# A 1-core transformer chain in fp32: more products by split operands, adaLN loads and accumulations moved

## The chip, the cores and the metric

The kernel runs on 1 core of one Trainium2 chip. Times are device microseconds of one execution; a result is the median of several.

## The reference, cut to what matters

One sequence of 256 tokens, width 1024, all in fp32. First come two layers conditioned on a vector `c`:

```
c_act = silu(c)
for layer in range(2):
    mod = c_act @ ada_w[layer] + ada_b[layer]          # 6 x 1024: shift, scale, gate for mixer and feed-forward
    h = rmsnorm(x) * (1 + scale_m) + shift_m
    mix = conv + retention(h) if layer == 0 else s5(h) # s5: two-way scan, GELU, then (z @ w_glu_a) * sigmoid(z @ w_glu_b)
    x = x + gate_m * mix
    h = rmsnorm(x) * (1 + scale_f) + shift_f
    x = x + gate_f * (relu(h @ w_fc1[layer]) ** 2 @ w_fc2[layer])
x = rmsnorm(x)
```

Then a block with three branches: `proj = rmsnorm(x) @ w_in` gives queries, keys, values and gates for gated linear attention (`gq, gk, gv, gg, ga1`), forgetting attention (`fq, fk, fv, ff`) and attention into a memory (`mq`), and three 1024-wide sigmoid gates `bg`; the gated branches are summed, go through `w_out`, and a SiLU-gated feed-forward of width 2816 follows.

## The kernel before, in words

Activations lie transposed, 1024 features as 8 tiles of 128 partitions by 256 tokens. Weights stream in panels of 2 MB (512 columns of all 1024 rows, or 512 rows of 1024 columns) through a ring of three slots, loaded by SP in the order of `panels`; a panel's load waits until TensorE has finished the panel three before it. TensorE works off one list of jobs, `job_order` (L62), in that order. Jobs write into six PSUM banks in turn, so a job waits until the job six before it has been read; the `ada` jobs share one further bank.

There are two ways to multiply. `project` (L1678) uses plain fp32 operands. `project_split` (L1716) uses operands cut in two fp32r parts, and `three` (L1710) sums high x high, high x low and low x high. For it a *unit* of a panel (128 x 2048 values, half a panel) is cut: ACT copies it into one of three high buffers (`split_high`, L778), VectorE subtracts and leaves the low part in the ring (`split_low`, L1232). A high buffer is free again when the unit three before it has been multiplied, which `split_high` waits for. Before, layer 0's first product (`f1.0.0` to `f1.0.15`), the first two of eight row blocks of its second (`FC2 = 2`, `rows_open`, L1695) and all projections of the last block are plain; the other row blocks (`rows_split`, L1728), GLU, layer 1's feed-forward, the branch outputs and the last feed-forward are split.

Conditioning: `mod` needs 24 column pieces k of `ada_w`, 2 MB each (k = 0 to 11 for layer 0, k = 12 to 23 for layer 1). `ada_load` (L576) brings piece k into one of two slots, from ACT's queue save the first two, which GpSimd issues. `ada_acc(k)` (L1176) multiplies its eight slabs by `c_act` and sums them on VectorE, eight instructions. TensorE's job `ada(k)` (L1759) sums over partitions, and `ada_mod(k)` (L1192) adds the bias into `mod`. `begin` (L1637) makes `ada(k)` wait until `mod` of k-1 is written. Where pieces fall is set by `ADA_AFTER` (L59): pieces 10 to 21 among the 16 jobs of layer 0's first product, 22 and 23 in its second (`side_work`, L1908).

S5 weights are prepared ahead: for each of eight groups GpSimd computes powers (`powers`, L647; 32 operations, then a store), TensorE's jobs `wt{k}.0`, `kl{k}`, `wt{k}.1` (`s5_weights`, L1860) turn them, ACT stores them (`s5_weights_out`, L855). GpSimd begins group k when `wt{k-1}.1` is done. Groups 1 to 4 stand in the first product, 5 to 7 in the second.

Every engine follows its own fixed order and stops at a wait. The orders that the change touches, on VectorE: start (L1258: `ada_acc` 0 to 3, norm, `ada_acc(4)`, `s5_scalars` at L1148, `gated` L1267, `convolve` L1271, `ada_acc(5)`), the adaLN loop of layer 0 (L1358), the loop over row blocks (L1362), the GLU loop (L1433), and in the last block the chain of decays (L1476 to L1506, ended by the job `kot`), `head_norm` (L1508), `gla_out` (L1538) and the eight attention rounds (L1566: logits, maximum, exp on ACT, normalisation). On ACT: `next_ada` (L891), the loop over row blocks (L898), `head_squares` (L1019), `gate` (L1048). In each round TensorE does `us{u}` (logits), a gate unit `bg{u}`, and the transpose `ut{u-1}`; every second round `uo` (values).

Of the kernel before, what the change touches and what calls it, by code (L numbers as in the profile page):

```python
# [20 lines left out]
P = 128  # L21
# [21 lines left out]
SW_ADA = 2  # L43
# [15 lines left out]
ADA_AFTER = {1: 10, 2: 11, 3: 12, 5: 13, 6: 14, 7: 15, 9: 16, 10: 17, 11: 18, 13: 19, 14: 20, 15: 21}  # L59


def job_order():  # L62

    jobs = ["ada0", "ada1", "ada2", "ms0", "ada3", "av0", "ag0", "av1", "ag1", "ada4", "q0", "q1", "cv0", "ada5", "k0", "k1", "ada6",
# [3 lines left out]
    for j in range(16):  # L68
        jobs.append(f"f1.0.{j}")
        if j in ADA_AFTER:  # L70
            jobs.append(f"ada{ADA_AFTER[j]}")
        if j % 4 == 0:
            k = j // 4 + 1
            jobs += [f"wt{k}.0", f"kl{k}", f"wt{k}.1"]
    for b in range(8):
        if b < 2:
            jobs.append(f"ada{22 + b}")
        if b % 3 == 0:
            k = 5 + b // 3
            jobs += [f"wt{k}.0", f"kl{k}", f"wt{k}.1"]  # L80
# [10 lines left out]
    jobs += ["ga0", "ga1", "gb0", "gb1", "ga2", "ga3", "gb2", "gb3", "ms3", "mk0", "mk1"]  # L91
    jobs += ["f1.1.0", "mkr0", "f1.1.1", "mkr1"] + [f"f1.1.{j}" for j in range(2, 16)]
    jobs += [f"f2.1.{p}" for p in range(4)] + ["ms4", "mv0", "ms5", "mv1"]
    jobs += ["gq0", "gk0", "ga1r", "ff", "gv0", "gv1", "la", "gg0", "gg1", "fq0", "fq1", "kot", "cs0", "cs1",
# [34 lines left out]
def build(nc, a, out):  # L129

    ctx = ExitStack()
    with ctx:
# [5 lines left out]
        def s(name):  # L138
            if name not in sems:
# [8 lines left out]
                   ("memory_kv", 2048), ("tabw", 3072), ("ada_acc", 1024)]  # L148
# [12 lines left out]
        prep = sb("prep", 3200)  # L161
# [115 lines left out]
        gates = big3  # L277
# [6 lines left out]
        wsm = early[:, 0:640].rearrange("p (k c) -> p k c", k=8)  # L284
        wa2 = early[0:16, 640:896]
# [88 lines left out]

        base = 0
        FC2 = 2
# [7 lines left out]
        add_units([f"f2.1.{i}" for i in range(8)], 512, high_bufs)  # L384
        base = BRANCH = len(units)
        high_bufs = [split["ada_slot0"][:, 0:2048], split["ada_slot0"][:, 2048:4096], split["big"][:, 24 * T:32 * T]]
# [9 lines left out]
        def unit_parts(u):  # L396

            name, c0, n, buf = units[u]
# [3 lines left out]
            return panel_view(name)[:, :, c0:c0 + n], low[:, :, c0:c0 + n], buf[:, 0:k * n].rearrange("p (k c) -> p k c", k=k)  # L402
# [11 lines left out]
        h_hi = split["squares"][:, :].rearrange("p (k t) -> p k t", k=KT)  # L414
        h_lo = split["h_in"][:, :].rearrange("p (k t) -> p k t", k=KT)
        big_lo = split["big"][:, :].rearrange("p (k t) -> p k t", k=32)

        def fc2_high(b):

            name, o = (("squares", 0), ("squares", 1024), ("memory_kv", 0))[(b - FC2) % 3]  # L420
            return split[name][:, o:o + 1024].rearrange("p (k t) -> p k t", k=4)
# [45 lines left out]
        freed.update({"gq0": ("gqk", 1), "gk0": ("gqk", 2), "ga1r": ("ga1c", 1), "ff": ("ffx", 1), "la": ("lax", 2),  # L467
# [14 lines left out]
        def unit_wait(eng, u):  # L482
# [8 lines left out]
            elif BRANCH <= u < LAST:  # L491
                job_wait(eng, branch_ends[u - BRANCH])
            else:
                first, before = (0, 0) if u < GLU else (SECOND + 16, 7 - FC2) if u < BRANCH else (DOWN, 14 - FC2)
# [4 lines left out]

        last_jobs = [name for name in JOBS if name[:2] in ("fg", "fu")]  # L500
        NORM_G = (("norm_g", 0), ("norm_g", 8), ("norm_g", 16), ("norm_g", 24), ("norm_f", 0), ("g_mix", 0), ("g_ffn", 0))
        NCONST = 6
        NLATE = 8

# [4 lines left out]
        def _(sp):  # L509
            sp.dma_start(cols[:, :], a["cols"]).then_inc(s("cols_in"), 16)  # L510
            sp.dma_start(x, a["x"].rearrange("(k p) t -> p k t", p=P)).then_inc(s("x_in"), 16)

            def load_win(k):
                if k == 0:
                    sp.wait_ge(s("ada_acc"), 2 * ADA)
# [23 lines left out]
            for i, (name, src, k, n, _) in enumerate(panels):  # L539
# [44 lines left out]

        @block.gpsimd
        def _(pool):
            pool.dma_start(prep[:, 0:192], a["s5_scal"]).then_inc(s("s5_in"), 16)
            ada_load(pool, 0)
            ada_load(pool, 1)
            pool.dma_start(ident[:, :], a["ident"]).then_inc(s("const_in"), 16)  # L590
# [23 lines left out]
            pool.dma_start(early[:, 1536:2176], a["rope"]).then_inc(s("const_in"), 16)  # L614
            pool.dma_start(scanmask[:, :], a["scanmask"]).then_inc(s("const_in"), 16)
            pool.dma_start(dreg[:, :], a["decay"]).then_inc(s("const_in"), 16)
            pool.dma_start(s5c[:, :], a["s5_select"]).then_inc(s("const_in"), 16)
# [114 lines left out]
        def _(act):  # L732
# [28 lines left out]
            def shift(n):  # L761

                act.wait_ge(s("mod"), ADA * (n // 2) + (2 if n % 2 == 0 else 8))
                for k in range(KT):
# [3 lines left out]
                    if n == 3 and k:  # L768
                        input_high(k - 1, s("h"), 24)
                if n == 3:  # L770
                    input_high(KT - 1, s("h"), 24)

            def input_high(k, ready, base):

                act.wait_ge(ready, base + k + 1)
                act.activation(h_hi[:, k, :], h[:, k, :], ACT.Copy).then_inc(s("h_high"), 1)

            def split_high(u):  # L778
# [4 lines left out]
                if u == 0:  # L783
                    job_wait(act, "f1.0.15")
                elif u in (1, 2):
# [7 lines left out]
                elif BRANCH <= u < BRANCH + 3:  # L793
# [82 lines left out]
            ada_load(act, 10)  # L876
            squares(1)
            ada_load(act, 11)
            shift(1)

# [10 lines left out]
            def next_ada(j):  # L891
                if j in ADA_AFTER:
                    ada_load(act, ADA_AFTER[j] + 2)
                if j % 4 == 0:
                    s5_weights_out(j // 4 + 1)

            relus(0, next_ada)
            for b in range(FC2, 8):  # L898
                for u in range(2 * (b - FC2), 2 * (b - FC2) + 2):
                    split_high(u)  # L900
                    if u == 2:
                        s5_weights_out(5)
# [4 lines left out]
                if b == FC2 + 2:  # L907
                    s5_weights_out(6)
            s5_weights_out(7)
# [46 lines left out]

            act.dma_start(wsm[:, :, 0:64], a["w_fox_f"].rearrange("(k p) c -> p k c", p=P)).then_inc(s("late"), 16)
# [4 lines left out]
            for p in range(4):  # L962
# [3 lines left out]
                act.activation(tmp3[:, 2 * p:2 * p + 2, :], ps2(f"gb{p}"), ACT.Sigmoid).then_inc(s("glus"), 1)  # L966
            split_high(SECOND)
# [9 lines left out]
            def after_relu(j):  # L977
                split_high(SECOND + j + 3)
                if j == 1:
                    root("mkr0", 512)  # L980
                    root("mkr1", 512)
                act_high(j, 2 * j, s("fsq"), j + 1)
# [1287 lines left out]
```

## Time and profile before

| what | us |
|---|---|
| median of 3 runs | 1395.38 |
| the runs | 1390.31, 1395.38, 1395.55 |
| the profiled execution | 1394.85 |
| its span | 1393.0 |
| TensorE busy | 1269.5 |
| VectorE busy | 735.4 |
| ACT busy | 452.9 |
| GpSimd busy | 370.1 |

The profile is of one execution. PE is TensorE's matmul side, PEld its weight loads, DVE VectorE, POOL GpSimd, SP the queue that loads panels. L1676 is the one line through which nearly all matmuls go, so stages are told apart by time and by the operands' names. A plain fp32 multiplication leaves two records, a split one three.

### The profile page before, as it was taken

What the parts mean: (1) busy time and instruction counts of PE and PEld (TensorE: products, weight loads), DVE (VectorE), ACT (ScalarE), POOL (GpSimd) and SP (SyncE); (2) the same over time, 40 slices, a digit from 0 to 9 for tenths busy, and PEclk for the clock granted to TensorE, in tenths of its full rate; (3) what the DMA queues carried; (4) which work ended last, traced back from release to release, by engine and by line L of the source; (5) the groups of instructions that cost most, each with busy time, mean ns of one, the idle gap of its engine ahead of it and who ended that gap; (6) DMA issues with size and microseconds to landing.
All of it is one profiled execution on the core that took longest, in us unless ns stands there. A gap on an engine that the chain in (4) does not pass through costs nothing.

```text
span 1393.0 us, 22876 instructions
## 1 busy us (share of the span) xinstructions
PE 1269.5 (91%) x9992; PEld 1135.4 (82%) x9992; DVE 735.4 (53%) x878; ACT 452.9 (33%) x619; POOL 370.1 (27%) x581
## 2 busy tenths in 40 slices
PE   1699998888999967888999999999999998899999
PEld 1587687777889947878999999668678898799998
DVE  4897985434363438955586543304542165555353
ACT  2221123111123343434555332114155343444341
POOL 7999653455534607810000000000000011000000
PEclk9899999999999988999999999999999999999999
DMA  8963675897765283426245555333333344355461
GB/s 324 365 216 140 226 258 203 328 340 289 280 228 210 100 314 107 130 73 235 100 175 183 186 186 183 109 108 126 113 122 121 121 149 154 121 182 182 143 220 61
DMA packets 118787, 258.08 MB, mean 185 GB/s; under 512 B 5056, under 2 KB 18656, under 8 KB 118560
## 3 DMA queue, kind: packets, MB, share of 16 engines
q1 hardware_dynamic: 86160, 185.78, 37.9%
q10 hardware_dynamic: 27584, 51.01, 10.0%
q0 software_dynamic: 4944, 19.83, 3.9%
q8 instruction: 79, 1.29, 0.4%
q14 instruction: 20, 0.16, 0.0%
HBM read 241.93 MB, written 14.68 MB: 184 GB/s over the span
## 4 chain that ended last, share of the span: by engine, by line
PE 71%; DVE 12%; DMA 8%; issue 3%; POOL 3%; ACT 3%; ACTq 0%; DVEq 0%; POOLq 0%
PE bank L1676 71%; DMA ada_slot<-in_ada_w 6%; DVE ada_acc L1189 3%; DVE big L1285 3%; POOL big L722 2%; DVE rstd L1199 1%; DMA memory_kv<-s_tables 1%; POOL big L715 1%; DVE ring_split L1236 1%; DVE h_in L1220 1%; ACT ada_slot_split L802 1%; DMA ring<-in_w_ffn_up 1%; DMA ring<-in_w_ffn_down 1%; DMA ring<-in_w_glu_a 1%; DVE ada_acc L1186 0%
## 5 line engine op out<-in xcount | busy, mean ns | idle before, releaser
L1676 PE MATMUL bank<-h_in,ring 128*128 128x256 f32 x1536 | 351.4, 390 | 7.7 <-ACT h_in L767 7.7
L1676 PEld LDWEIGHTS bank<-h_in,ring 128*128 128x128 f32 x1536 | 297.7, 195 | 53.3 <-issue 10.7
L1676 PE MATMUL bank<-squares_split,ring_split 128*128 128x256 f32 x800 | 226.9, 284 | 0.0
L728 POOL TENSOR_TENSOR y_cat<-y_cat,tmp 128x512 f32<-128x512 f32 x8 | 10.7, 1345 | 552.4 <-DVE tmp L1608 552.4
L1676 PEld LDWEIGHTS bank<-squares_split,ring_split 128*128 128x128 f32 x800 | 154.1, 193 | 0.0
L1189 DVE SCALAR_TENSOR_TENSOR ada_acc<-ada_slot,cact,ada_acc 128x512 f32<-128x512 f32 x168 | 134.0, 797 | 5.9
L1676 PE MATMUL bank<-ada_slot_split,ring_split 128*128 128x256 f32 x432 | 122.2, 283 | 0.0
L1236 DVE TENSOR_TENSOR ring_split<-ring,ada_slot_split 128x2048 fp32r<-128x2048 f32 (+1 forms) x24 | 53.9, 2247 | 62.6 <-ACT ada_slot_split L802 62.6
L1676 PEld LDWEIGHTS bank<-ada_slot_split,ring_split 128*128 128x128 f32 x432 | 82.9, 192 | 0.0
L1676 PE MATMUL bank<-h_in_split,ada_slot_split 128*128 128x256 f32 x256 | 74.9, 293 | 8.3 <-DVE y_cat_split L1612 3.8
L1676 PE MATMUL bank<-one,ada_acc 128*128 128x1 f32 x192 | 29.1, 273 | 56.4 <-DVE mod L1194 35.3
L1199 DVE RECIPROCAL rstd<-bank 128x512 f32<-128x512 f32 (+1 forms) x21 | 56.0, 2669 | 43.8 <-ACT bank L746 43.4
L1676 PEld LDWEIGHTS bank<-one,ada_acc 128*128 128x128 f32 x192 | 29.7, 229 | 59.8 <-DVE mod L1194 37.6
L1236 DVE TENSOR_TENSOR ring_split<-ring,tabw_split 128x2048 fp32r<-128x2048 f32 x22 | 50.4, 2291 | 50.2 <-ACT tabw_split L802 50.2
L885 ACT ACTIVATE big<-bank 128x512 f32<-128x512 f32 x32 | 19.1, 598 | 167.2 <-PE bank L1676 167.2
L802 ACT ACTIVATE ada_slot_split<-ring 128x2048 fp32r<-128x2048 f32 (+1 forms) x24 | 44.9, 1876 | 67.6 <-PE bank L1676 41.5
L1676 PE MATMUL bank<-squares_split,tabw_split 128*128 128x256 f32 x208 | 59.0, 284 | 0.0
L1676 PE MATMUL bank<-h_in_split,tabw_split 128*128 128x256 f32 x208 | 58.9, 283 | 0.0
L1676 PEld LDWEIGHTS bank<-h_in_split,ada_slot_split 128*128 128x128 f32 x256 | 51.1, 199 | 9.4 <-issue 8.2
L1676 PE MATMUL bank<-h_in_split,ring_split 128*128 128x256 f32 x192 | 56.1, 292 | 0.0
L1186 DVE TENSOR_SCALAR ada_acc<-ada_slot,cact 128x512 f32<-128x512 f32 x24 | 12.1, 503 | 82.9 <-DMA ada_slot<-in_ada_w 82.9
L802 ACT ACTIVATE tabw_split<-ring 128x2048 fp32r<-128x2048 f32 x22 | 42.0, 1911 | 41.8 <-PE bank L1676 31.7
(391 smaller groups left out, 3084.7 us busy)
## 6 DMA issues: line engine op xcount, KB each, us to landing
ring<-in_w_fc SPq DMA_DIRECT2D x32, 2048.0 KB, 8.2
ada_slot<-in_ada_w ACTq DMA_DIRECT2D x22, 2048.0 KB, 12.4
ring<-in_w_in SPq DMA_DIRECT2D x19, 2048.0 KB, 8.1
ring<-in_w_ffn_gate SPq DMA_DIRECT2D x5, 2048.0 KB, 7.7
ring<-in_w_ffn_up SPq DMA_DIRECT2D x5, 2048.0 KB, 7.8
ring<-in_w_ffn_down SPq DMA_DIRECT2D x5, 2048.0 KB, 7.9
ring<-in_w_out SPq DMA_DIRECT2D x4, 2048.0 KB, 9.1
ring<-in_w_branch SPq DMA_DIRECT2D x3, 2048.0 KB, 7.9
```

Source lines behind the costliest of these rows:

```text
L715: pool.tensor_tensor(wbuf[n % 2], pb[:, 0], pb[:, 1], ALU.add).then_inc(s("s5w"), 1)
L722: pool.tensor_tensor(rotated(m)[:, 1], gbuf[m % 2][:, :, ::-1, :], tab[:, :, 2:0:-1, :], ALU.mult).then_inc(s("s5r"), 1)
L728: pool.tensor_tensor(merged, merged, tmp3[:, 2 * p:2 * p + 2, :], ALU.add).then_inc(s("mga"), 1)
L802: act.activation(high, whole, ACT.Copy).then_inc(s("w_high"), 1)
L885: act.activation(hh, ps2(f"f1.{l}.{j}"), ACT.Relu).then_inc(s("relu"), 1)
L1186: ts(acc, w[:, 0, :], cact[:, 0:1], None, ALU.mult).then_inc(s("ada_part"), 1)
L1189: stt(acc, w[:, i, :], cact[:, i:i + 1], acc, ALU.mult, ALU.add)\
L1199: return dve.reciprocal(rs[:, 0:width], ps(job)[:, 0:width]).then_inc(s(sem), 1)
L1220: stt(dst[:, k, :], x[:, k, :], gain[:, k:k + 1], rs[:, 0:T], ALU.mult, ALU.mult).then_inc(s("hn"), 1)
L1236: tt(low, whole, high.bitcast(F32), ALU.subtract).then_inc(s("w_low"), 1)
L1285: stt(conv[:, i, :], src, w, conv[:, i, :], ALU.mult, ALU.add).then_inc(s("conv"), 1)
L1676: return pe.matmul(*args, skip_group_check=True, **kw)
```

## The change

1. Layer 0's first product and all projections of the last block become split units, the second product leaves one row block plain (`FC2 = 1`). The norms in front of them (`SPLIT_NORMS`) are cut too. `ga1r` and `ff` become one job of 80 rows.
2. The first four adaLN pieces are loaded by SP ahead of the first panel, into the two slots, a part of `big` and ring slot 2; VectorE accumulates six of their slabs, TensorE two. Small loads (`s5_scal`, constants) move from GpSimd's queue to SP's. `ms0` goes ahead of `ada0`.
3. The other pieces are spread: 10 to 15 in the first product, accumulated in halves, 16 to 20 in the second, 21 in GLU, 22 and 23 in layer 1. S5 groups stand after jobs 0, 5, 10, 15 and row blocks 1, 3, 5.

```diff
-SW_ADA = 2
+EARLY_ADA = 4
+DVE_SLABS = 6
...
-ADA_AFTER = {1: 10, 2: 11, 3: 12, 5: 13, 6: 14, 7: 15, 9: 16, 10: 17, 11: 18, 13: 19, 14: 20, 15: 21}
+ADA_AFTER = {3: 10, 6: 11, 8: 12, 11: 13, 13: 14, 15: 15}
+ADA_LOAD_AFTER = {2: 12, 5: 13, 7: 14, 10: 15, 12: 16, 14: 17}
+ADA_HALVES = {0: (10, 0), 1: (10, 1), 2: (11, 0), 4: (11, 1), 5: (12, 0), 6: (12, 1), 7: (13, 0), 9: (13, 1),
+              10: (14, 0), 11: (14, 1), 12: (15, 0), 13: (15, 1)}
+ADA_MOD_BEFORE = {5: 10, 8: 11, 10: 12, 13: 13, 15: 14}
+S5_AFTER = {0: 1, 5: 2, 10: 3, 15: 4}
+SIDE_ADA = {0: 16, 1: 17, 3: 18, 5: 19, 6: 20}
+SIDE_S5 = {1: 5, 3: 6, 5: 7}
...
-        FC2 = 2
+        FC2 = 1
+        T_, B_, Y_ = buffers_at((("tmp", 0), ("big", 6144), ("y_cat", 0)))
+        for i in range(16):
+            units.append((f"f1.0.{i // 2}", 256 * (i % 2), 256, ((T_, B_, Y_) * 4 + (T_, Y_) * 2)[i]))
...
+            for k in range(EARLY_ADA):
+                sp.dma_start(ada_slot(k), ada_source(k)).then_inc(ada_in(k)[0], 16)
...
+                elif u < FC:
+                    job_wait(act, f"f1.0.{u - 3 if u < 13 else u - 2}")
...
-            squares(0, False)
-            for k in range(2, 6):
-                ada_load(act, k)
-            root("ms0")
+            squares(0)
+            act.wait_ge(s("panel0"), 16)
+            ada_load(act, 4)
             shift(0)
+            ada_load(act, 5)
             ada_load(act, 6)
...
             def next_ada(j):
-                if j in ADA_AFTER:
-                    ada_load(act, ADA_AFTER[j] + 2)
-                if j % 4 == 0:
-                    s5_weights_out(j // 4 + 1)
+                if j + 3 < FC:
+                    split_high(j + 3)
+                if j in ADA_LOAD_AFTER:
+                    ada_load(act, ADA_LOAD_AFTER[j])
+                if j in S5_AFTER:
+                    s5_weights_out(S5_AFTER[j])
...
             for b in range(FC2, 8):
                 for u in range(2 * (b - FC2), 2 * (b - FC2) + 2):
-                    split_high(u)
-                    if u == 2:
-                        s5_weights_out(5)
+                    split_high(FC + u)
+                    if u in (4, 8, 12):
+                        s5_weights_out(4 + u // 4)
...
                 act.activation(fc2_high(b), big3[:, 4 * b:4 * b + 4, :], ACT.Copy).then_inc(s("b_high"), 1)
...
+                if 3 <= b < 6:
+                    ada_load(act, 15 + b)
...
             def head_squares(i, name, dst):
...
+                split_high(PROJ + (9, 10, 11, 12, 15, 16)[i])
...
             def gate(j):
...
+                if GATES + j + 3 < BRANCH:
+                    split_high(GATES + j + 3)
...
+            split_low(0)
             residual(0, "wo0", 16)
...
-            for k in range(10, 23):
-                ada_acc(k)
-                if k > 10:
-                    ada_mod(k - 1)
+            for j in range(16):
+                if j + 3 < FC:
+                    split_low(j + 3)
+                if j in ADA_MOD_BEFORE:
+                    ada_mod(ADA_MOD_BEFORE[j])
+                if j in ADA_HALVES:
+                    k, half = ADA_HALVES[j]
+                    ada_acc(k, 4 * half, 4 * half + 4)
+            ada_acc(16)
+            ada_mod(15)
             for b in range(FC2, 8):
-                split_low(2 * (b - FC2))
-                split_low(2 * (b - FC2) + 1)
+                split_low(FC + 2 * (b - FC2))
+                split_low(FC + 2 * (b - FC2) + 1)
...
+                if b == 1:
+                    ada_acc(17)
+                    ada_mod(16)
+                elif b == 2:
+                    ada_acc(18)
+                    ada_mod(17)
+                elif b == 4:
+                    ada_mod(18)
+                    ada_acc(19)
+                elif b == 5:
+                    ada_acc(20)
+                    ada_mod(19)
...
+                if p == 1:
+                    ada_acc(21)
+                if p == 2:
+                    ada_mod(21)
...
+            for u in range(5, 9):
+                split_low(PROJ + u)
             dve.wait_ge(s("ffe"), 2)
...
+                split_low(GATES + u + 3)
...
             for u, name in enumerate(glu_jobs):
                 project_split(name, GLU + u, z_hi, z_lo, (lambda k: pe.wait_ge(s("z_low"), k + 1)) if u == 0 else no_wait)
+                if name == "ga3":
+                    ada(21)
```

## Rows read from the trace of the kernel before

**Rows 1.** Waits of TensorE: engine, line, releaser: us in total, times, longest.

```profile
PE bank L1676 <- DVE mod L1194: 35.3, 7, 11.7
PE bank L1676 <- DVE ada_acc L1189: 21.1, 2, 18.7
```

**Rows 2.** Chain that ended last: start us, us, what, number of records.

```profile
632.57 23.48 PE bank L1676 x192
...
1090.49 8.64 PE bank L1676 x40
...
1326.08 63.60 PE bank L1676 x528
```

**Rows 3.** Windows of three stages: length, PE, PEld, DVE, ACT, POOL busy (records), clock, DMA, GB/s.

```profile
226.40:385.80 159.40, 144.14 (x993) 125.49 (x994) 74.16 (x115) 27.52 (x51) 77.39 (x136) 0.93 0.82 297
385.80:497.20 111.40, 110.92 (x1010) 105.38 (x1011) 50.26 (x45) 34.54 (x30) 50.27 (x67) 0.97 0.48 175
888.50:1122.00 233.50, 230.22 (x1018) 178.49 (x1018) 74.32 (x104) 83.46 (x134) 0.00 (x0) 0.99 0.34 117
```

**Rows 4.** Timeline of VectorE at the start: start us, us, line, operation.

```profile
59.73 0.52 DVE L1186 TENSOR_SCALAR ada_acc<-ada_slot,cact 128x512 f32<-128x512 f32 x1
60.28 5.59 DVE L1189 SCALAR_TENSOR_TENSOR ada_acc<-ada_slot,cact,ada_acc 128x512 f32<-128x512 f32 x7
...
75.60 0.69 DVE L1269 TENSOR_TENSOR big<-bank,big 128x512 f32<-128x512 f32 x1
```

**Rows 5.** The page: bytes moved by slice, DMA issues with us to landing.

```profile
GB/s 324 365 216 140 226 258 203 328 340 289 280 228 210 100 314 107 130 73 235 100 175 183 186 186 183 109 108 126 113 122 121 121 149 154 121 182 182 143 220 61
...
ring<-in_w_fc SPq DMA_DIRECT2D x32, 2048.0 KB, 8.2
ada_slot<-in_ada_w ACTq DMA_DIRECT2D x22, 2048.0 KB, 12.4
```

**Rows 6.** Groups by form of ACT and VectorE: busy us, mean ns, idle before.

```profile
L802 ACT ACTIVATE y_cat_split<-ring 128x2048 fp32r<-128x2048 f32 x15 | 28.7, 1912 | 27.1 <-PE bank L1676 27.1
...
L885 ACT ACTIVATE big<-bank 128x512 f32<-128x512 f32 x32 | 19.1, 598 | 167.2 <-PE bank L1676 167.2
...
L1236 DVE TENSOR_TENSOR ring_split<-ring,y_cat_split 128x2048 fp32r<-128x2048 f32 x15 | 34.5, 2297 | 24.8 <-ACT y_cat_split L802 24.8
```

**Rows 7.** Timeline of VectorE: norm of layer 1, reciprocal and last low parts.

```profile
667.10 1.76 DVE L1199 RECIPROCAL rstd<-bank 128x256 f32<-128x256 f32 x1 [6.11 <-ACT bank L746]
...
675.84 0.76 DVE L1230 TENSOR_TENSOR h_in_split<-h_in,squares_split 128x256 fp32r<-128x256 f32 x2 [0.55 <-ACT squares_split L776]
```

**Rows 8.** Timeline of TensorE in layer 0's first product, behind an adaLN job.

```profile
264.44 9.31 PE L1676 MATMUL bank<-h_in,ring 128*128 128x256 f32 x32
```

**Rows 9.** Chain that ended last, ahead of the S5 scan.

```profile
499.26 16.59 DMA memory_kv<-s_tables
```

**Rows 10.** Timeline of GpSimd: ends of a step, operations that meet other work.

```profile
160.40 1.12 POOL L655 TENSOR_TENSOR tabw<-tabw,early 128x128 f32<-128x128 f32 x2
...
236.60 0.54 POOL L674 DMA_DIRECT2D memory_kv<-in_s_bc  x1 [19.74 <-PE bank L1676]
...
257.09 0.58 POOL L707 DMA_DIRECT2D s_wout<-prep  x1 [0.30 <-POOL prep L660]
...
450.34 2.81 POOL L655 TENSOR_TENSOR tabw<-tabw,early 128x128 f32<-128x128 f32 x2
```

**Rows 11.** Timeline of VectorE in GLU.

```profile
641.85 2.29 DVE L1236 TENSOR_TENSOR ring_split<-ring,ada_slot_split 128x2048 fp32r<-128x2048 f32 x1 [5.28 <-ACT ada_slot_split L802]
```

**Rows 12.** Timeline of ACT around the chain of decays.

```profile
938.50 0.60 ACT L1004 ACTIVATE big<-bank 128x512 f32<-128x512 f32 x1 [6.31 <-PE bank L1676]
...
953.29 0.60 ACT L1030 ACTIVATE tmp<-bank 128x512 f32<-128x512 f32 x1
```

**Rows 13.** Timelines of VectorE and ACT in one attention round.

```profile
1046.70 0.69 DVE L1574 TENSOR_TENSOR tabw<-bank,early 128x512 f32<-128x512 f32 x1 [4.02 <-PE bank L1676]
...
1049.46 1.28 ACT L1052 ACT_TABLE_LOAD   x1
```

More of the change, by code:

```diff
@@ L90, in job_order @@
     jobs.append("z7")
-    jobs += ["ga0", "ga1", "gb0", "gb1", "ga2", "ga3", "gb2", "gb3", "ms3", "mk0", "mk1"]
-    jobs += ["f1.1.0", "mkr0", "f1.1.1", "mkr1"] + [f"f1.1.{j}" for j in range(2, 16)]
+    jobs += ["ga0", "ga1", "gb0", "gb1", "ga2", "ga3", "ada21", "gb2", "gb3", "ms3", "mk0", "mk1"]
+    jobs += ["f1.1.0", "mkr0", "f1.1.1", "mkr1"]
+    for j in range(2, 16):
+        jobs.append(f"f1.1.{j}")
+        if j in (5, 9):
+            jobs.append(f"ada{22 + j // 9}")
     jobs += [f"f2.1.{p}" for p in range(4)] + ["ms4", "mv0", "ms5", "mv1"]
-    jobs += ["gq0", "gk0", "ga1r", "ff", "gv0", "gv1", "la", "gg0", "gg1", "fq0", "fq1", "kot", "cs0", "cs1",
+    jobs += ["gq0", "gk0", "ff", "gv0", "gv1", "la", "gg0", "gg1", "fq0", "fq1", "kot", "cs0", "cs1",
              "nr0", "nr1", "at0", "at1", "fk0", "fk1", "go0", "gor0", "nr2", "nr3", "go1", "gor1",
@@ L160, in build @@
         early = sb("early", 2176)
-        prep = sb("prep", 3200)
+        prep = plain["prep"]
         s5c = sb("s5_select", 656)
@@ L284, in build @@
         wsm = early[:, 0:640].rearrange("p (k c) -> p k c", k=8)
+        wsm_hi, wsm_lo = (split[name][:, o:o + 640].rearrange("p (k c) -> p k c", k=8) for name, o in (("tabw", 2048), ("prep", 2048)))
         wa2 = early[0:16, 640:896]
@@ L981, in after_relu @@
                     root("mkr1", 512)
+                if j == 4:
+                    act.wait_ge(s("late"), 80)
+                    act.activation(wsm_hi, wsm, ACT.Copy).then_inc(s("wsm_high"), 1)
+                if j == 3:
+                    ada_load(act, 23)
+                if j == 8:
+                    act.wait_ge(s("ada_acc"), 24)
                 act_high(j, 2 * j, s("fsq"), j + 1)
             relus(1, after_relu)
-            for u in range(SECOND + 19, BRANCH):
+            for u in range(SECOND + 19, PROJ):
                 split_high(u)
             squares(4)
+            split_high(PROJ)
             job_wait(act, "mv0")
@@ L1183, in ada_acc @@
                     dve.wait_ge(s("cact"), 1)
-                for i in range(KT):
+                for i in range(first, min(end, n)):
                     if i == 0:
@@ L1552, in _ @@
             gla_out(1)
+            for u in range(13, 16):
+                split_low(PROJ + u)
             def fox_rows(hd):
@@ L1786, in _ @@
             pe.wait_ge(s("pool_const"), 6)
-            ada(0)
-            ada(1)
-            ada(2)
             mean_squares(0)
-            ada(3)
+            for k in range(EARLY_ADA):
+                ada(k)
             w, w_ag = panel("av"), panel_view("ag")
```

320 lines of the change are left out of this document (210 added, 110 removed).

## The prediction

> **What bounds the kernel now.** I first read who TensorE waits for [rows 1]: the adaLN vectors (`DVE mod` and `DVE ada_acc`, 56.4 us together) are its largest waits. Next, its pace between waits, from the chain that ended last [rows 2]: 40 records of plain fp32 take 8.64 us, 0.216 each, and a multiplication leaves two, so a 256-column unit (16 multiplications, 32 records) takes 6.91 us; a split one is 48 records of 63.60 / 528 = 0.1205 us, 5.78 us. A conversion gives back 1.13 us a unit. The windows of the stages [rows 3] show layer 0's first product idle for 15.3 us and at 0.93 of the clock, with DMA at 0.82; the second product and block 2's projections have no idle time to speak of. So TensorE bounds nearly everything, save the start (adaLN, then VectorE's convolution) and the S5 scan.
>
> The sum is against the profiled execution, 1394.85 us (span 1393.0 and 1.85 around it), 0.5 us under the median shown.
>
> **Start.** Four adaLN loads go ahead of the first panel on SP's queue, and TensorE takes two of eight slabs of each. What decides is VectorE: ada4's accumulation (6.1 us), S5 scalars, gated values, 46 convolution steps, ada5, which TensorE waits for. Before, that chain starts at 59.73 and reaches the gated values at 75.60 [rows 4]. Now ada4's load is issued when `av` has landed: 11.9 MB are ahead, 33 us at the 365 GB/s of the second slice; 12.4 us for a load beside others [rows 5] gives 46 and the gated values at about 62: **-13** (-8 if loads behind each other are slower, -16 if they land at once). ACT waits for ada4 inside its queue (load 6) until then, with `ag0`'s sigmoid behind it, which is needed only after it. Constants and S5 scalars move from GpSimd's queue to SP's; they are needed 20 us later.
>
> **Into layer 0's feed-forward.** One `split_low`, 2.3 us [rows 6], stands ahead of the residual that frees the bank of `wo0.3`: +2.3. The normed input is now split: in layer 1 the same code goes from reciprocal to last low part in 667.10 to 676.6 [rows 7], so the first job ends 13.4 us behind `ms1`, not 10.8: +2.6. Together **+4.9**.
>
> **Layer 0's products.** Fifteen further units give 15 x 1.13 = 17.0, the converted block (64 fp32 records to 96 split ones) 2.2, three adaLN jobs of 0.85 that move out 2.5: **-21.7**. The old waits and their slow clock go: 15.3 idle, 0.07 x 159 and 0.03 x 111 for the clock [rows 3], **-30**. The unit behind such a wait took 9.31 us, where 6.91 is the pace: behind an idle TensorE the granted clock is the lower of its two levels, 1.2 of 2.4 GHz, for part of the stretch [rows 3, 8]; I count 2.4 us a wait below.
>
> New waits come from order, not load. TensorE's `ada(k)` needs `mod` of k-1 read. VectorE reads it in step j only behind `split_low(j+3)`, whose high half ACT makes after job j: relu 0.6, a square as long, split 1.9, then low 2.3 and the small read, 5.6 us [rows 6]. `ada12` stands directly behind job 8 and mod 11 is read in step 8: 5.6 us. `ada13` stands behind job 11, mod 12 in step 10 behind unit 13, whose buffer only frees after job 11: 1.9 + 2.3 + 0.2 = 4.4. `ada14` stands behind job 13, mod 13 behind unit 15, free after job 13, and half an accumulation (3.1): 7.5. Sum 17.5, and 3 x 2.4 of clock.
>
> The second product has a larger one. VectorE accumulates ada18 after block 2's parts, but ACT issues its load only at the end of its block 3, whose second unit waits for the first half of TensorE's block 2. From there: 1.9 + 1.1, load 8 to 12 [rows 5], accumulation 6.1 [rows 4], `split_low` 2.3: 20 to 23 us, while TensorE has 5.8 us left. Block 3 waits **14.7**, plus 2.4 clock. ada19 and ada20 have a block more in hand: 1.5. New waits: 17.5 + 7.2 + 14.7 + 2.4 + 1.5 = **+43.3**. The net of this stage is only -8.4.
>
> **S5.** Its weights end one block earlier, so its tables no longer queue behind each other; the table that landed after 16.6 us [rows 9] arrives before ACT needs it: **-4.3** (0 if still queued).
>
> GpSimd makes those weights in 20.5 us a step, 236.60 to 257.09; by the sums above the steps now stand 26 to 43 us apart. Two of its operations that meet a `split_low` take 2.81 us, the same two under back-to-back convolution steps 1.12 [rows 10]: about 2 us for each split. So a step with four to five splits takes about 29: **+3.5** over three places (0 to 10). The Trainium skill (Trainium Architecture — The Big Picture, "What this means for kernel authors") calls the port pair of VectorE and GpSimd an exclusive lock, not a shared bandwidth. By that a step would stretch by all of VectorE's busy time and the sum would be 42 us higher; The 1.12 speaks against so strict a reading, the 2.81 for it with long instructions.
>
> **GLU.** `ada21` stands behind `ga3` on TensorE, and its accumulation behind `split_low` of unit 6, whose panel lands late: that split ends at 644.1 [rows 11], gating 2.0, accumulation 6.2: 652.3, with TensorE ready two units after 632.57 [rows 2], at 644.3. +8.0, the job 0.8, clock 2.2: **+11**. ada22 and ada23 cost 1.6 and about 1 of lag in layer 1: **+2.6**.
>
> **Projections and gates.** 22 units give 24.9; the four token-major jobs have 512 columns, for which the trace has no split row: between 0.216 (one fp32 record of 256) and 0.241 (twice 0.1205), 5.2 to 5.8 a job against 6.91; I take 5.3, the column rate, -6.4; `ga1r` and `ff` merge, 7.2 to 2.9. Together **-36** (bounds -38 and -33). Against it:
> - the split input and first units, 1.7;
> - decay chain: `kot` was ready just in time, 13 us after `gg1`; ACT ran from 938.50 to `kot`'s copy at 953.29 [rows 12]. Now a split precedes the exponentials and two more precede that copy, 5.7, and TensorE has 2.3 us less work to cover it: 8 less the 0.6 there was, about 6 with rounding by the splits that overlap;
> - `mq1`, whose unit frees after `fv0`: 1.4;
> - the eight attention rounds. Logits to the end of exp take 2.8 us (1046.70 to 1049.46), the sigmoid table 1.3 [rows 13], sigmoids 0.8. Now ACT's split 1.9 and VectorE's 2.3 come between the gate and the next logits: 9.1 a round, 9.8 with the forget rows, 14 with the head norms; TensorE needs 7.9 to 9.3. Over the eight some 10.5.
>
> So **+19.6**, net -16.4.
>
> Sum: -13 + 4.9 - 8.4 - 4.3 + 3.5 + 11 + 2.6 - 16.4 = -20.1, so **1374.5 us**.
>
> On the pace: the Trainium skill (TensorE: Matmul & The Clock Gate, "Wait — 56ns, not 53.3ns?") gives back-to-back matmuls N / 2.4 GHz plus 2.5 ns, 109 ns at 256 columns. By it the sum would be about 22 us lower; 528 matmuls at 120.5 ns [rows 2] decide.
>
> **Rivals.**
> - *No new waits.* ACT and VectorE stay ahead everywhere: 43.3, 10, 1, 19.6 and 3.5 us less, 1297. For it: VectorE is at 32% in the projections [rows 3]. Against it: each wait is an order in a queue, not a load. 7%.
> - *The projections keep TensorE's pace*, the rest as forecast: 1355. The rounds have three converted units in hand, and overlap may hide more than I count. 15%.
> - *DMA decides the start and the first product.* Its 0.82 share [rows 3] stays about as high with shorter jobs; loads issued two jobs ahead (ada13, ada15) come late and the start gains 8: 1374.5 + 5 + 12, 1391. 12%.
> - *GpSimd falls behind* (slower). If every VectorE instruction holds it off as the long splits do [rows 10], a step takes 20 us plus VectorE's busy time, 38 to 45, and TensorE waits at steps 2, 3, 4, 5 and 7 for 13, 8, 2, 10 and 12: +45 for my 3.5, **1416**. It passes the old time once it costs 24 us and is measurably slower from 31. It is the lock of the skill's page named above, taken literally. 10%.
> - That the conversion doesn't change the pace: the rows of split units stand beside it, so I give it nothing.
> The forecast itself has 56%, with 1360 to 1389 as its own range.
>
> **Numbers.** Measurements of this kernel can tell about 0.5%, 7 us, from no change. The range leaves out the first rival and most of the slower one: 1338 to 1396. Faster 0.78 (forecast and the first two rivals), same 0.12, slower 0.10.
>
> **What would show it.** TensorE waits for `mod` three times in the first product, once some 15 us for a `ring_split` in the second, 8 us for `ada_acc` after `ga3`; ada5's end near 98; a round in the gates near 9 to 10 us; PE records of 0.12 us throughout. The prediction is wrong if block 3 starts at once, if the rounds run at 8 us, or if `ident`/`prep` work on TensorE waits for POOL `tabw` or `prep` in the first product.

## The result and the profile after

The changed kernel takes 1404.49 us (median of 5 runs, 1403.93 to 1408.42) against 1394.29 for the kernel before on the same chip: the ratio is 1.0081, 95% interval 1.0061 to 1.0101. It is **slower by 0.8%**, where 1374.5 us was forecast. The profiled execution took 1404.07 us, its span is 1402.1.

The top of the page of the changed kernel: busy time and instructions, then the clock granted in 40 slices.

```profile
PE 1240.2 (88%) x10720; PEld 1157.7 (83%) x10720; DVE 840.4 (60%) x932; ACT 538.4 (38%) x681; POOL 405.6 (29%) x573
...
PEclk7889998989897898989799999999998999999999
```

TensorE is busy 29.3 us less than before (1269.5), so the conversions did their work; but its idle time grew from 123.5 to 161.9 us. VectorE has 105 us more to do. Who TensorE waits for, over the whole span (us in all, times, longest):

```profile
PE bank L1822 <- DVE mod L1290: 24.1, 7, 7.2
PE bank L1822 <- POOL prep L714: 17.8, 3, 9.1
PE bank L1822 <- DVE ada_acc L1285: 17.4, 3, 10.1
PE bank L1822 <- ACT squares L811: 17.3, 4, 8.7
PE bank L1822 <- DVE big_split L1476: 16.3, 2, 15.5
```

Against [rows 1] the adaLN vectors cost less (41.5 us for 56.4), but two waits are new: for GpSimd's S5 weights (`POOL prep`) and for the cut activations of a row block (`DVE big_split`). Stage by stage, from the ends of TensorE's jobs in the two traces (`ms` jobs sum the squares for a norm; each row ends with the job named), what came on top of the kernel before or fell away, in us:

| stretch | forecast | measured |
|---|---|---|
| start to `ada5` | -13 | -5.6 |
| to `ms1` (retention, `wo0`) | +2.3 | +6.3 |
| to the end of `f1.0.0` (cut norm) | +2.6 | +2.9 |
| to `f2.0.3` (layer 0's products) | -4.9 | +15.8 |
| to `z7` (S5) | -4.3 | -6.5 |
| to `gb3` (GLU) | +11 | +12.7 |
| to `mv1` (layer 1) | +2.6 | +1.8 |
| to `bg11` (projections and gates) | -16.4 | -18.7 |
| rest | 0 | +0.3 |
| sum | -20.1 | +9.0 |

The table holds the whole miss. Layer 0's products are 20.7 us off, the start 7.4, the way into the feed-forward 4; the other stages came as forecast. The windows of the changed kernel from `ms1` to `f2.0.3`, of the projections and gates, and of a stretch in which TensorE does nothing (length, busy us of PE, PEld, DVE, ACT, POOL, then clock, DMA share and GB/s):

```profile
223.50:516.50 293.00, 236.70 (x2266) 230.81 (x2266) 164.99 (x160) 96.15 (x108) 168.82 (x203) 0.88 0.64 230
915.90:1130.70 214.80, 199.11 (x1394) 179.92 (x1394) 132.39 (x136) 128.15 (x162) 0.00 (x0) 0.96 0.36 128
424.00:434.50 10.50, 0.00 (x0) 0.00 (x0) 10.25 (x11) 0.00 (x0) 6.97 (x9) 0.51 0.57 234
```

and the first of them in the kernel before:

```profile
222.80:497.10 274.30, 254.96 (x2001) 230.82 (x2002) 127.32 (x161) 63.16 (x83) 127.66 (x203) 0.95 0.68 249
```

Between `ms1` and `f2.0.3` TensorE is busy 18.3 us less and idle 37.0 us more (56.3 for 19.3). The waits in that stretch are these:

```profile
PE bank L1822 <- POOL prep L714: 17.8, 3, 9.1
PE bank L1822 <- DVE mod L1290: 17.4, 3, 7.2
PE bank L1822 <- DVE big_split L1476: 16.3, 2, 15.5
PE bank L1822 <- DVE h_in_split L1328: 4.8, 1, 4.8
```

**Theory:** the conversion is a gain on TensorE, and the waits that come with it, each with one cause in some engine's order, more than eat it in layer 0. **Rivals:** the stage is bound by VectorE or GpSimd, so that a wait mended comes back at the next job; or the conversion itself gains less than the records say.

### The profile page after: what moved, and what is told of

The parts are those of the page before. It is cut to its first block, busy times and chain, and to the rows that moved or that the text cites. A ratio compares the mean times of both kernels' runs of the same rounds, so it can differ in the third digit from the quotient of the medians.

```text
span 1402.1 us, 24511 instructions
## 1 busy us (share of the span) xinstructions
PE 1240.2 (88%) x10720; PEld 1157.7 (83%) x10720; DVE 840.4 (60%) x932; ACT 538.4 (38%) x681; POOL 405.6 (29%) x573
## 3 DMA queue, kind: packets, MB, share of 16 engines
q8 instruction: 85, 1.39, 0.4%
## 4 chain that ended last, share of the span: by engine, by line
PE 62%; DVE 13%; POOL 10%; DMA 6%; issue 4%; ACT 4%; SPq 1%; DVEq 0%; POOLq 0%; ACTq 0%
PE bank L1822 62%; DVE big L1385 3%; DVE ada_acc L1285 3%; DMA ada_slot<-in_ada_w 3%; POOL tabw L709 3%; DVE rstd L1295 2%; POOL tabw L706 2%; DVE ring_split L1334 2%; POOL big L776 2%; DMA ring<-in_w_in 1%; POOL prep L714 1%; POOL big L769 1%; SPq L580 1%; POOL tabw L714 1%; DMA ring<-in_w_ffn_up 1%
## 5 line engine op out<-in xcount | busy, mean ns | idle before, releaser
L1822 PE MATMUL bank<-squares_split,ring_split 128*128 128x256 f32 x1056 | 304.4, 288 | 0.0
L1822 PEld LDWEIGHTS bank<-squares_split,ring_split 128*128 128x128 f32 x1056 | 208.8, 198 | 0.0
L1822 PE MATMUL bank<-big_split,ring_split 128*128 128x256 f32 x352 | 100.3, 285 | 0.0
L1822 PE MATMUL bank<-squares_split,tmp_split 128*128 128x256 f32 x240 | 74.5, 310 | 5.6 <-DVE h_in_split L1328 4.8
L1334 DVE TENSOR_TENSOR ring_split<-ring,y_cat_split 128x2048 fp32r<-128x2048 f32 x22 | 51.6, 2344 | 46.0 <-ACT y_cat_split L868 45.9
L1334 DVE TENSOR_TENSOR ring_split<-ring,tmp_split 128x2048 fp32r<-128x2048 f32 x20 | 48.0, 2401 | 48.8 <-ACT tmp_split L868 48.8
L1822 PE MATMUL bank<-h_in,ring 128*128 128x256 f32 x320 | 74.4, 396 | 1.7 <-ACT h_in L821 1.7
L1822 PE MATMUL bank<-squares_split,y_cat_split 128*128 128x256 f32 x208 | 60.7, 292 | 15.5 <-DVE big_split L1476 15.5
L1822 PEld LDWEIGHTS bank<-h_in,ring 128*128 128x128 f32 x320 | 63.7, 200 | 11.0 <-issue 1.7
L1822 PEld LDWEIGHTS bank<-big_split,ring_split 128*128 128x128 f32 x352 | 68.2, 194 | 0.0
L1822 PE MATMUL bank<-one,ada_acc 128*128 128x1 f32 x192 | 31.0, 283 | 36.7 <-DVE mod L1290 19.3
```

The costliest lines, as they stand in the source:

```text
L1334: tt(low, whole, high.bitcast(F32), ALU.subtract).then_inc(s("w_low"), 1)
L1822: return pe.matmul(*args, skip_group_check=True, **kw)
```

## The experiments

Twelve kernels ran, each a change of the changed kernel. Times of one experiment stand against 1404.5 us; each ratio is to the kernel before, run beside it on the same chip. The experiments ran on four chips, on which the kernel before took 1392.2 to 1394.3 us, so a difference in us between two of them can be off by some 2 us. The traces add as much: the stretch of the last block from `ms5` to the norm of its feed-forward takes 292 to 295 us in runs whose edits don't touch it.

### e1: pieces 18 to 20 loaded a row block earlier

```diff
-                if 3 <= b < 6:
-                    ada_load(act, 15 + b)
+                if 2 <= b < 5:
+                    ada_load(act, 16 + b)
```

> Theory (order in queues): block 3 of layer 0's second product waited 15.5 us because ACT issues the load of piece 18 only at the end of its block 3, behind a unit that waits for TensorE. Issued at the end of ACT's block 2 (and 19, 20 a block earlier too), the load lands before VectorE asks for it, the 15.5 us go and about 2 us of low clock with them: 1387 us. Rival (the next late thing takes the place: GpSimd's weights of groups 6 and 7, or the copy of block 3's second unit): at most 6 us gained, 1398 us.

Measured: 1391.02 us, ratio 0.9980 (0.9964 to 0.9996). The waits between `ms1` and `f2.0.3`:

```profile
PE bank L1822 <- DVE mod L1290: 17.5, 3, 7.2
PE bank L1822 <- POOL prep L714: 15.9, 3, 6.8
...
PE bank L1822 <- DVE big_split L1476: 3.8, 3, 3.1
```

The three loads, moved by one line, give back 13.5 us, and the changed kernel no longer loses to the one before. `ada18` ends 16 us earlier; then `kl6` waits 6.8 us for GpSimd, which it hadn't, `kl7` no longer waits (9.1 before), and row block 6 waits 3.1 for its cut activations. So the rival is right for a part, the theory for most.

### e2: `mod` read ahead of `split_low` in the same step

```diff
             for j in range(16):
-                if j + 3 < FC:
-                    split_low(j + 3)
                 if j in ADA_MOD_BEFORE:
                     ada_mod(ADA_MOD_BEFORE[j])
+                if j + 3 < FC:
+                    split_low(j + 3)
```

> Theory: the three waits for mod in layer 0's first product (17.4 us in sum) come only from reading mod behind split_low in VectorE's step. With the read ahead of it they go, with about 1.5 us of low clock each: 17.4 + 4.5 less, 1382 to 1386 us. Rival (VectorE is the bound of this stage, busy 44 of 64 us, and the units' low halves come late instead): 8 us or less gained, 1396 us or more.

Measured: 1401.03 us, ratio 1.0058 (1.0041 to 1.0076): 3.5 us less, where 18 or more were expected. In the trace the stage itself is 5.8 us shorter. The waits for `mod` in the first product fell only from 17.4 in three to this:

```profile
PE bank L1822 <- DVE mod L1290: 12.2, 2, 8.8
```

`ada13`'s wait went. The other two stayed for what stands a step earlier in VectorE's order: the trace of e2 has, ahead of the read at 304.42, the last half accumulation, and ahead of that the `split_low` of the step before.

```profile
298.62 2.35 DVE L1334 TENSOR_TENSOR ring_split<-ring,big_split 128x2048 fp32r<-128x2048 f32 x1 [0.42 <-ACT big_split L868]
300.90 0.95 DVE L1282 TENSOR_SCALAR ada_acc<-ada_slot,cact 128x512 f32<-128x512 f32 x1
301.89 2.61 DVE L1285 SCALAR_TENSOR_TENSOR ada_acc<-ada_slot,cact,ada_acc 128x512 f32<-128x512 f32 x3
304.42 0.15 DVE L1290 TENSOR_TENSOR mod<-bank,cols 128x4 f32<-128x4 f32 x1
```

The read has to stand a whole step earlier; e8 does that.

### e3: `ada21` behind `gb3`

```diff
-    jobs += [..., "ga2", "ga3", "ada21", "gb2", "gb3", "ms3", "mk0", "mk1"]
+    jobs += [..., "ga2", "ga3", "gb2", "gb3", "ada21", "ms3", "mk0", "mk1"]
...
-                if p == 2:
+                if p == 3:
                     ada_mod(21)
```

> Theory: in GLU TensorE waits for the accumulation of piece 21 because its job stands between ga3 and gb2. Behind gb3 it costs its own 0.8 us: about 9 us less (7.5 of wait, 2 of clock), 1395 us. Rival: the accumulation, 6.2 us on VectorE, still stands ahead of the low halves of the last units, so gb2 and gb3 wait for those: 3 us or less gained, 1401 us.

Measured: 1401.44 us, ratio 1.0070 (1.0048 to 1.0091). In GLU the wait for the accumulation (6.4) went, and the waits for low halves grew from 1.9 to this:

```profile
PE bank L1822 <- DVE ring_split L1334: 4.9, 2, 2.5
```

From the end of `f2.0.3` to the end of `gb3` the trace is 8.3 us shorter, though 0.8 of that is `ada21`, which now comes behind; the span is only 3.5 shorter, since the start took 1.2 and the last block 2.7 us longer, which the edit doesn't touch. So the stage bears out the theory for most of its 9 us, and the time alone can't tell it from the rival.

### e4: constants behind `q`'s panel

```diff
-                if name == "ag":
+                if name == "q":
                     sp.dma_start(ident[:, :], a["ident"]).then_inc(s("const_in"), 16)
```

(the four other constants with it; 1864 KB in all)

> Theory: the start gained 5.6 us where 13 were forecast because the load of piece 4 shares the DMA queues with 1.86 MB of constants that moved ahead of it; behind q's panel they leave 1.86 MB / 386 GB/s = 4.8 us: piece 4 lands near 48.5 instead of 53.2, ada5 ends near 100 instead of 105, 1399.7 us. Rival (loads queue behind ag's panel alone, the constants being small packets that fill gaps): 1 us or less.

Measured: 1402.91 us, ratio 1.0081 (1.0062 to 1.0100). The median doesn't resolve it. In the trace the load of piece 4 takes 13.6 us from issue (36.17) to landing (49.79), against 18.1 in the changed kernel, and `ada5` ends 3.3 us earlier against `ada0`: the constants' share is there, some 3 to 4 us.

### e5: each `split_low` in four pieces

```diff
-                tt(low, whole, high.bitcast(F32), ALU.subtract).then_inc(s("w_low"), 1)
+                k = whole.shape[1]
+                n = min(4, k)
+                for i in range(n):
+                    rows = slice(k * i // n, k * (i + 1) // n)
+                    part = tt(low[:, rows, :], whole[:, rows, :], high[:, rows, :].bitcast(F32), ALU.subtract)
+                part.then_inc(s("w_low"), 1)
```

> Each split_low is four subtractions of a quarter instead of one of 2.3 us. Theory (a GpSimd operation waits for the VectorE instruction in flight): six operations of group 2's step that take 2.6 to 3.3 us beside a split_low drop to 1.0 to 1.7, the step from 36.3 to about 30 us, TensorE's waits for GpSimd from 17.8 to about 5, 1392 us. Rival (VectorE's busy time in sum holds GpSimd off, however it is cut): the step stays at 36, the waits at 17.8, 1402 to 1405 us.

Measured: 1407.22 us, ratio 1.0103 (1.0076 to 1.0130). GpSimd's step for group 2, its first and its last row, in the changed kernel:

```profile
240.21 0.54 POOL L728 DMA_DIRECT2D memory_kv<-in_s_bc  x1 [26.02 <-PE bank L1822]
...
276.51 0.60 POOL L761 DMA_DIRECT2D s_wout<-prep  x1 [0.30 <-POOL prep L714]
```

and in e5:

```profile
242.63 0.54 POOL L728 DMA_DIRECT2D memory_kv<-in_s_bc  x1 [28.32 <-PE bank L1827]
...
272.10 0.60 POOL L761 DMA_DIRECT2D s_wout<-prep  x1 [0.30 <-POOL prep L714]
```

36.3 us became 29.5, as the theory has it, and TensorE's waits for GpSimd between `ms1` and `f2.0.3` fell from 17.8 to 1.6. But the time is no better than the rival's 1402 to 1405. A unit cut in quarters beside GpSimd's step takes VectorE 3.2 to 3.9 us, where the one long instruction of the changed kernel took 2.3 to 2.8:

```profile
259.19 3.86 DVE L1338 TENSOR_TENSOR ring_split<-ring,y_cat_split 128x512 fp32r<-128x512 f32 x4
```

so TensorE waits for VectorE instead:

```profile
PE bank L1827 <- DVE big_split L1481: 23.6, 3, 16.6
PE bank L1827 <- DVE mod L1290: 23.4, 3, 10.0
```

What GpSimd won, VectorE lost for the larger part, as if the two engines took one resource in turn. In this trace, the fastest of the four runs, the stage is 4.0 us shorter all the same, and the start (1.5) and the last block (2.2) take that back.

### e6 and e7: one conversion undone

e6 takes the projections and gates back to plain fp32, e7 layer 0's first product. The core of e7 (e6 has `PROJ <= u < BRANCH` for `u < FC`, and 5 for 1):

```diff
-        SPLIT_NORMS = (1, 3, 5, 6)
+        SPLIT_NORMS = (3, 5, 6)
...
             def split_low(u):
+                if u < FC:
+                    return
...
             def project_split(name, u, x_high, x_low, ready):
+                if u < FC:
+                    i = place[units[u][0]]
+                    pe.wait_ge(s(f"panel{i % RING}"), 16 * (i // RING + 1))
+                    whole = unit_parts(u)[0]
+                    return project(name, whole, 0, h, h_ready(1) if ready is not no_wait else no_wait)
```

> The last block's projections and gates are plain fp32 again, with nothing cut for them (ga1r and ff stay one job); all else as in the changed kernel. Theory: from us0 to bg11 and before it the conversion gave the stage 18.7 us less ga1r's 4.3: 1404.5 + 14 to 19 = 1419 to 1423 us. Rival (the gain is the merged job and shifted waits): 1410 us or less.

> Layer 0's first product is plain fp32 again, with nothing cut for it; the spread of adaLN pieces and S5 groups stays. Theory: its conversion saves 16 x 1.13 = 18 us of multiplications and brings the waits for mod (17.4, and 4.5 of clock), GpSimd's at kl2 (5.4 and 1.3), the cut norm (2.6) and the split_low ahead of the residual (3.3 and 1.3): 36 us. Plain it is then about 18 us faster, 1386 us. Rival (the waits come from the spread loads, and the conversion is a gain that they hide): 18 us slower than the changed kernel less the 7 us of the input, 1416 us.

Measured: e6 1421.45 us, ratio 1.0201 (1.0172 to 1.0229), 17 us slower than the changed kernel. e7 1383.82 us, ratio 0.9945 (0.9927 to 0.9964), **20.7 us faster** than the changed kernel (19 by the two ratios) and faster than the one before. So one conversion was worth 17 us, and the other cost some 20, though it saves TensorE the same 1.13 us a unit. In e7 the wait for `mod` is gone from the stage, and GpSimd's at `kl2` too (the other two, at the second product, stay):

```profile
PE bank L1827 <- DVE big_split L1481: 16.3, 2, 15.4
PE bank L1827 <- POOL prep L714: 12.4, 2, 9.1
```

e7 also shows GpSimd's step for group 2 with VectorE idle (VectorE has nothing between 240.5 and 260.9):

```profile
239.50 0.54 POOL L728 DMA_DIRECT2D memory_kv<-in_s_bc  x1 [25.28 <-PE bank L1827]
...
258.80 0.60 POOL L761 DMA_DIRECT2D s_wout<-prep  x1 [0.30 <-POOL prep L714]
```

19.3 us alone, 36.3 beside 29.6 us of VectorE. That is what the first product's conversion does to GpSimd.

### e8 and e9: the waits mended together

e8 has e1, e3 and e4; `mod` read ahead of `split_low` and a step earlier; unit 0's `split_low` ahead of piece 9's accumulation; and piece 4's load without the wait for `av`'s panel. e9 is e8 without this last part.

```diff
-ADA_MOD_BEFORE = {5: 10, 8: 11, 10: 12, 13: 13, 15: 14}
+ADA_MOD_BEFORE = {4: 10, 7: 11, 9: 12, 12: 13, 14: 14}
...
             for k in range(7, 10):
+                if k == 9:
+                    split_low(0)
                 ada_acc(k)
...
-            split_low(0)
             residual(0, "wo0", 16)
...
-            act.wait_ge(s("panel0"), 16)
             ada_load(act, 4)
```

> Together: pieces 18 to 20 loaded a block earlier, mod read a step earlier and ahead of split_low, ada21 behind gb3, constants behind q's panel, piece 4's load without the wait for av's panel, split_low of unit 0 ahead of piece 9's accumulation. Theory: 13 (piece 18) + 20 (mod) + 8 (GLU) + 5 and 4 (start) + 4 (residual) = 54 less, of which faster TensorE gives about 10 back at GpSimd's weights: about 1360 us. Rival (VectorE and GpSimd are the bound of layer 0's feed-forward, so each wait taken away comes back at the next job): 1380 us or more.

> The kernel with six waits mended, but piece 4 is loaded behind av's panel again. Theory: its early load took the DMA queues from piece 3 and av's panel (ada3 ended 6.1 us and av0 8.4 us later than in the changed kernel) and so gave nothing; behind the panel ada5 ends 1.5 to 3 us earlier, about 1359 us. Rival (only VectorE's chain counts here, the order of the loads doesn't): no change, 1361 us.

Measured: e8 1361.03 us, ratio 0.9761 (0.9736 to 0.9786); e9 1362.12, ratio 0.9758 (0.9733 to 0.9783). e8 is 43.5 us faster than the changed kernel, as the theory had it (about 1360). The waits of e9 between `ms1` and `f2.0.3`:

```profile
PE bank L1823 <- POOL prep L714: 15.9, 3, 6.7
PE bank L1823 <- DVE h_in_split L1328: 4.8, 1, 4.8
PE bank L1823 <- DVE big_split L1477: 3.9, 3, 3.1
PE bank L1823 <- DVE mod L1290: 2.6, 1, 2.6
```

The waits of order are gone, 33.7 us down to 6.5; GpSimd's is left. On piece 4 the rival held: in e8 it delays piece 3 and so the norm, in e9 it lands late itself, and its accumulation begins at 52.9 and 50.7.

### e10: GpSimd given more room

```diff
-S5_AFTER = {0: 1, 5: 2, 10: 3, 15: 4}
+S5_AFTER = {0: 1, 6: 2, 11: 3, 15: 4}
-SIDE_S5 = {1: 5, 3: 6, 5: 7}
+SIDE_S5 = {1: 5, 4: 6, 6: 7}
```

(on e9; in ACT's order the stores of groups 6 and 7 move with them)

> As e9, and S5 groups 2 and 3 stand a job later in the first product, 6 and 7 a row block later in the second. Theory: GpSimd needs 33 to 36 us for a step beside VectorE, so TensorE's waits at kl2 (5.9) and kl6 (7.1) with their clock go, 2 to 3 us come at kl7: 11 us less than e9, 1348 us. Rival (the sum of the steps is the bound, the waits only move to the next step and to the S5 tables): 4 us or less.

Measured: 1346.88 us, ratio 0.9673 (0.9655 to 0.9690), 15.2 us less than e9; the stage between `ms1` and `f2.0.3` accounts for 12.3 of it in the traces, and 2.9 lie in the last block. The wait for GpSimd is down to a third, 3.5 us are back at a row block:

```profile
PE bank L1824 <- DVE big_split L1478: 7.4, 2, 7.0
...
PE bank L1824 <- POOL prep L714: 4.6, 1, 4.6
```

So the sum of GpSimd's steps is not the bound; where they stand is.

### e11: e9 with the first product plain

The edit is that of e7 on e9.

> As e9, with layer 0's first product plain. Theory: with the waits for mod mended the conversion of this product is a gain, but a small one: plain adds 18 us of multiplications and takes away GpSimd's wait at kl2 (5.9 and 1.3), the rest of ada14's (2.6 and 1.5) and the cut norm (2.6): 4 us slower than e9, about 1363 us. Rival (the conversion is worth its full 18 us once mod is read in time): 1377 us.

Measured: 1362.87 us, ratio 0.9773 (0.9753 to 0.9793), against e9's 0.9758: the same. With `mod` read in time the conversion of the first product neither gains nor loses within the intervals; TensorE waits 10.0 us for GpSimd in e11's stretch and 15.9 in e9's, and for a shorter time on the norm; that takes what it saves in work.

### e12: piece 4 ahead of `ag`'s panel

```diff
-            act.wait_ge(s("panel0"), 16)
-            ada_load(act, 4)
...
+                if name == "ag":
+                    ada_load(sp, 4)
                 sp.dma_start(panel_view(name), src).then_inc(s(f"panel{i % RING}"), 16)
```

(on e10)

> As e10, and piece 4 is loaded by SP between av's and ag's panels, not by ACT behind av's landing. Theory: the start missed its forecast because piece 4 landed at 53.2 (50.7 with the constants behind q), 9 and 6.6 us after VectorE had nothing else to do; it now lands near 41, VectorE goes on at 44, ada5 ends near 95.5 instead of 101.8: 6 us less, 1341 us. Rival (ag's panel, 5.4 us later, or GpSimd's table work beside the same VectorE instructions take it back): 2 us or less.

Measured: 1344.46 us, ratio 0.9656 (0.9630 to 0.9682); the interval overlaps e10's, so the time is unclear. The trace shows the step: VectorE begins piece 4 at

```profile
44.48 0.48 DVE L1283 TENSOR_SCALAR ada_acc<-ada_slot,cact 128x512 f32<-128x512 f32 x1
```

and `ada5` ends at 95.0 instead of 101.8. `mu`, the mean for the convolution's norm, is 11 us earlier; then TensorE waits at `kl0` for GpSimd, which has only moved its bound:

```profile
PE bank L1824 <- POOL prep L716: 5.2, 1, 5.2
```

4 to 6 us of the 11 are left behind it.

## Why the prediction was wrong

**Right.** The pace: a split unit takes 5.77 us in layer 1 of the changed kernel (48 records of 0.120). The waits for `mod`: 17.5 forecast, 17.4 measured, three times and where it said; but that each is a read behind `split_low` *of its own step* was right for `ada13` alone, the other two had a second cause a step earlier (e2). Block 3: 14.7 + 1.5 forecast, 16.3 measured, down to 3.8 with the loads moved (e1). S5, GLU, layer 1: within 2.2 us each. The -30 for the old waits: 15.3 us idle, and the jobs behind them took 13.3 us more than the same jobs elsewhere, where 14.5 was forecast for the clock. (A slip in the sum: 1394.85 less 20.1 is 1374.75, not 1374.5.)

**The step that failed: "So a step with four to five splits takes about 29: +3.5 over three places".** Layer 0's products came out 20.7 us worse. GpSimd's weights cost 17.8 us of waiting and 4.8 us of clock behind it, 22.6 where 3.5 stood: 19 of the 20.7.

- *GpSimd's step.* I charged 2 us for each of four or five `split_low` and let the other VectorE work pass. Beside group 2 stood six `split_low` and seventeen instructions of the adaLN accumulation. Single operations or pairs that met a split took 2.1 to 3.3 us for 0.6 to 0.8, and single ones that met an accumulation 0.95 to 1.07 for 0.62 to 0.74. The step took 36.3 us, not 29, and TensorE was there after 31. I had this mechanism as the slower rival with 10%, at 38 to 45 a step and +45 in all; the measured step lies between my two values, nearer the rival's. The Trainium skill (Trainium Architecture — The Big Picture, "What this means for kernel authors") has the two engines' ports under an exclusive lock. The runs agree that one engine's work holds the other up: alone the step takes 19.3 us, beside 29.6 us of VectorE 36.3, so GpSimd loses 0.57 of VectorE's time, and in e5 VectorE loses most of what GpSimd wins. They don't bear out the strict reading that I had worked out, all of VectorE's time, which would be 48.9 here. And e10, which gives the steps more room, brings e9's waits for GpSimd from 15.9 us to 4.6.
- *The clock behind the new waits*, 9.6 forecast (four times 2.4), about 16 measured, by the jobs behind each wait against the same jobs elsewhere: 9.4 behind the three for `mod` (7.2 forecast), 1.9 behind block 3 (2.4), and 4.8 behind GpSimd's three, for which the sum had nothing. At `kl2`, for one, a job of 0.65 us took 1.08:

```profile
276.26 1.08 PE L1822 MATMUL bank<-prep 128*32 128x64 f32 x32 [5.42 <-POOL prep L714]
```

Where the lower clock falls decides its price. Before, nearly all of it fell on work: one of the old waits, and what followed it, in the kernel before (columns as above):

```profile
299.19:302.92 3.73, 0.00 (x1) 0.02 (x1) 3.59 (x7) 1.23 (x2) 0.00 (x0) 1.00 1.04 402
302.94:309.77 6.83, 6.83 (x20) 5.84 (x21) 5.70 (x9) 0.00 (x0) 0.00 (x0) 0.50 1.05 390
```

In the changed kernel, in block 3's long wait, much of it fell on idle time (0.51 above). So the stage's 20.7 is 14.3 (GpSimd's waiting) and 6.5 (clock behind new waits) and 1.2 (old clock priced too high), less 1.3 by which, as what is left over, the work itself came out shorter.

**Start:** -13 forecast, -5.6 measured. The mis-sized term is "12.4 us for a load beside others": piece 4 was issued at 35.12, near the forecast 33, and landed 18.1 us later, so VectorE went on at 53.25 and reached the gated values at 69.11, not 62.

```profile
53.25 0.49 DVE L1282 TENSOR_SCALAR ada_acc<-ada_slot,cact 128x512 f32<-128x512 f32 x1 [9.33 <-DMA ada_slot<-in_ada_w]
...
69.11 0.68 DVE L1369 TENSOR_TENSOR big<-bank,big 128x512 f32<-128x512 f32 x1
```

Between issue and landing the DMA engines move 395 GB/s without a gap. What lands when is then a sum of bytes, and by an estimate from that rate `ag`'s panel (5.3 us) and the 1864 KB of constants (4.8) were ahead or beside. I had written that the constants are needed 20 us later, which is true of them and misses what they hold up. e12, with piece 4 ahead of both, has the forecast gain at `ada5`: 15.6 us against the kernel before. For the start, then, the third rival ("DMA decides", a gain of 8) was the nearer one; its waits for loads in the first product didn't come.

**Into the feed-forward:** +2.3 for the `split_low` ahead of the residual became 3.5, since `wo0.3` behind that wait took 10.1 us for 8.9; 2.1 more is `ada9`, whose load came only 2.8 us earlier while TensorE came 4.8 earlier. e9, with unit 0 split in an idle gap of VectorE, has `wo0.3` at 9.9 us again, as before.

**Projections:** -16.4 forecast, -18.7 measured; TensorE is busy 31.1 us less and idle 12.4 more [rows 3]. The rival that the rounds keep TensorE's pace was right for their larger part: from `bg3` to `bg8` a round takes 7.9 us, where the forecast had 9 to 10, and TensorE waits for nobody. That is one of the signs of a wrong prediction that it named itself; another, a wait for GpSimd's `prep` in the first product, came as well. The 512-column jobs take 5.6 us (six records of `gv` in 1.39 us, 0.232 each), where I took 5.3.

**Sum of the misses:** 20.7 + 7.4 + 4.0 + 0.3 (norm) + 1.7 (GLU) + 0.3 (rest), less 2.2 (S5), 0.8 (layer 1) and 2.3 (projections): 29.1, the distance between -20.1 and +9.0. The range ended at 1396 because GpSimd's wait was given 3.5 us beside a rival of 45, with nothing between; the measured cost lies in that gap.

## What to carry to other kernels

Where a conversion takes time off the engine that bounds, price it by what it puts in the other engines' queues: the same 1.13 us a unit was worth 17 us where only ACT and VectorE had to follow, and cost some 20 where small reads, loads and a GpSimd step stood in the same queues. Most of each of those waits went by moving a line or two, and with all of them the design that had lost 0.8% won 3.3% (e10). That doesn't make the first product's conversion a gain: e11 puts it at nothing in e9, and e10 without it was not run. And when VectorE's work grows beside a GpSimd step that TensorE waits for, count every VectorE instruction that overlaps it, and give the step room before its result is due.

## What was not expected

- Cutting VectorE's long subtraction in quarters shortens GpSimd's step by 6.8 us (36.3 to 29.5) and lengthens the subtraction beside it from at most 2.8 us to as much as 3.9: this kernel gained nothing by shorter instructions.
- The granted clock of a stretch without any matmul is shown as 0.51, so a low value beside idle time need not be slow work; in the old wait shown above it was the other way round, 1.00 in the wait and 0.50 over the work behind it.
- The conversion of a whole product can come out at nothing: in e11 TensorE is busy 10.1 us more than in e9 (1245.2 for 1235.1) and idle 8.6 us less, and the times agree within their intervals.
